# The squared activations of two MLPs turned by VectorE in 32x32 blocks instead of by TensorE

## The chip, the cores and the metric

One Trainium2 chip, one core. The metric is the device time of one execution in microseconds; of several runs the median is taken.

## The reference, cut to what matters

The program computes three transformer layers on 256 tokens of width 2048 in float32. The change lies in the MLPs of the first two layers, which have this form:

```python
def sq_relu_mlp(h, w1, w2):          # h: 256 x 2048, w1: 2048 x 8192, w2: 8192 x 2048
    a = jax.nn.relu(jnp.einsum("btd,df->btf", h, w1))
    return jnp.einsum("btf,fd->btd", a * a, w2)

# for each of two layers
x = x + rms_norm(m, mix_post_g[layer])        # m: output of the layer's mixer
h = rms_norm(x, ffn_pre_g[layer])
x = x + rms_norm(sq_relu_mlp(h, ffn_w1[layer], ffn_w2[layer]), ffn_post_g[layer])
```

Around them stand a pooling and convolution mixer (before the first MLP), a short convolution (between them), and a third layer with attention and gating (behind the second).

## The kernel before

All large products go the same way. The activations are the stationary operand, 128x128, with the features on the partitions; the weights are the moving operand, 128 rows x 512 columns; a product of 256 tokens x 512 columns is a *chunk* and fills two PSUM banks, one for each tile of 128 tokens. Both operands are kept as a sum of two fp32r parts, hi and lo, and each product is three matmuls: hi by lo, lo by hi and hi by hi (lines 687 to 689, `step_matmuls`). A chunk is worked in *steps* of two feature tiles, 12 matmuls each. There are 960 steps in one list, `SEQ`; `POS` gives a step's place in it and `S_END` the place behind a chunk's last step.

SyncE loads weights two steps at a time into three slots of w_raw. For each step ScalarE rounds the raw weights to w_hi (`split_hi`, line 666) and VectorE subtracts it from the raw ones into w_lo (`split_lo`, line 673). There are six slots for the split weights. Each engine has its own program, in which the steps of `SEQ` follow each other in a loop (`split_steps`); at step s ScalarE and VectorE first split the weights of step s+3, and then do what else belongs to step s. TensorE's loop (`matmul_steps`) waits for the split weights and for the stationary operand, issues the 12 matmuls, and then does what else belongs to the step.

An MLP goes in 8 blocks of 1024 hidden features. A block has two *up* chunks of 8 steps (j = 0, 1, with w1, stationary operand A) and four *down* chunks of 4 steps (with w2, stationary operand B). They are ordered so that the up chunks of block b+1 come ahead of the down chunks of block b: up 0, up 1, down 0, up 2, down 1, and so on, up 7, down 6, down 7. In block 0 the two up chunks are interleaved. For an up chunk

- ScalarE takes the banks at the chunk's last step, with the ReLU and the tokens' scale, into one of three slots of z (`to_z`, line 958): 128 tokens on the partitions, 512 features, for each of the two token tiles;
- GpSimd squares them in place (`pool_mlp`, line 1870);
- at the second step behind the chunk TensorE waits for the squares (`squared`) and turns them: eight transpositions of 128x128 by an identity (`turn_z` and `turn`, line 732), four into each of two of the four small PSUM banks, 4 to 7 (`aux_bank`); these are used in turn by every such piece of work of the program, in the order that `aux_order` lists, and TensorE waits for a bank to be free (`aux_free`);
- at the same step of their own programs ScalarE casts the two banks into B_hi (`hi_plain`, line 993), and VectorE, behind it, subtracts B_hi from the banks into B_lo (`lo_plain`, line 1353). A later `wait_step` of TensorE waits for `lo_cast`.

B has room for 16 feature tiles, so two blocks. Down chunks are added into `acc`: those of block 0 are copied by ScalarE (`copy_acc`), those of blocks 1 to 6 are added by VectorE at the chunk's last step (line 1633). The buffer `conv_out` is used by the mixers and by the attention, and by nothing in the MLPs.

Of the kernel before, what the change touches and what calls it, by code (L numbers as in the profile page):

```python
# [13 lines left out]
TOK = 256  # L14
# [25 lines left out]
Z_SLOTS = 3  # L40
TAP_SLOTS = 2
STEP_K = 2
AHEAD = 3
# [29 lines left out]
def up_chunk(layer, b, j):  # L73
    return (C_M0, C_M1)[layer] + (j if b == 0 else 2 + 6 * (b - 1) + j)
# [106 lines left out]

def aux_order():
    two = range(2)
    yield from [("first",)]
    yield from [("pre", 0, g, h) for g in range(NG) for h in two]
    yield from [("rows",)]
    yield from [("vg", q) for q in range(4)]
    for j in two:
        yield from [("win", j, h) for h in two] + [("mix", j, h) for h in two]
    yield from [("ln", tt, h) for tt in two for h in two]  # L190
    yield from [("silu", j, h) for j in two for h in two]
    for layer in two:
        yield from pre_fills(1 + 2 * layer)
        yield from [("h", layer, b, j, h) for b in range(NB) for j in two for h in two]
        if layer == 0:
            yield from pre_fills(2)
            for j in range(NG):
                yield from [("cu", j, h) for h in two] + [("bg", j, h) for h in two]
    yield from pre_fills(4)
    yield from [("qk", r, h) for r in range(4) for h in two]  # L200
    yield from [("ws", h) for h in two]
    for r in range(8, 14):
        for i in range(8):
            if (r, i) in ((11, 1), (13, 1)):
                yield from [("sgu", (r - 11) // 2, tt) for tt in two]
            if (r, i) == (12, 3):
# [29 lines left out]
def build(nc, t):  # L236
    ctx = ExitStack()
    with ctx:
# [6 lines left out]
        def signal(name, keys):  # L245
            return Signal(semaphore(name), list(keys))
# [23 lines left out]
        S0 = [POS[c, 0] for c in range(N_CHUNKS)] + [STEPS]  # L270
        S_END = [POS[c, n_steps[c] - 1] + 1 for c in range(N_CHUNKS)]
        STEPS_PER_LOAD = GK // STEP_K
        LOADS = STEPS // STEPS_PER_LOAD

# [43 lines left out]
        att = conv_out_flat[:, 0:NT * W_ATT].rearrange("p (t c) -> p t c", t=NT)  # L318
        vg = conv_in_flat[:, 0:NT * W_ATT].rearrange("p (t c) -> p t c", t=NT)
        ws_T = ws_flat.rearrange("p (g c) -> p g c", g=HEADS)  # L320
        scores = scores_flat.rearrange("p (s c) -> p s c", s=2)
# [49 lines left out]

        aux = list(aux_order())
        AUX_N = {k: n for n, k in enumerate(aux)}
        CAST = [k for k in aux if k[0] in ("pre", "mix", "silu", "h", "bg", "ao", "zb", "merged")]

# [27 lines left out]
        for p in range(4):  # L403
# [6 lines left out]
                                   ([(g, tt) for tt in tiles for g in gs] if 0 in gs else [(g, tt) for g in gs for tt in tiles])])  # L410
        tap_done = signal("tap_done", DVE_TAPS)
        ln_bias = signal("ln_bias", [(tt,) for tt in tiles])
        ln_stats = signal("ln_stats", [(tt, h) for tt in tiles for h in two])
# [36 lines left out]
        def aux_done(key):  # L450
# [3 lines left out]
            if kind == "rows":  # L454
                return par_made.sem, par_made.of("rows", 3)
            if kind in ("pre", "mix", "h", "ao", "zb", "merged"):
                return lo_cast.sem, lo_cast.of(*key)
# [21 lines left out]
        def z_done(key):  # L479
# [3 lines left out]
            if kind == "v":  # L483
                return aux_filled.sem, aux_filled.of("vg", *rest)
            by_pe = {"u": "win", "p": "mix", "c": "cu", "b": "bg", "qk": "qk", "ub": "zb", "h": "h", "ws": "ws"}
            if kind in by_pe:
# [145 lines left out]
        def since(c, i, before):  # L632

            return POS[c, i] - S_END[before]

# [81 lines left out]
        def pe_program(e):  # L717
# [102 lines left out]

            boundary(1)
            pe_mlp(e, turn_x, turn_z, 0)
            boundary(2)

# [12 lines left out]
            boundary(3)  # L837
            pe_mlp(e, turn_x, turn_z, 1)
            boundary(4)
# [68 lines left out]

        def pe_mlp(e, turn_x, turn_z, layer):
# [37 lines left out]
        def act_program(e):  # L947
# [150 lines left out]
            boundary(1)  # L1098
            act_mlp(e, at, to_z, hi_plain, copy_acc, squares, early, 0)
            boundary(2)  # L1100
# [31 lines left out]
            boundary(3)  # L1132
            act_mlp(e, at, to_z, hi_plain, copy_acc, squares, early, 1)
            boundary(4)


            for c, i in split_steps(e, 4, split_hi, at):
                r = c - C_L2
                if i == n_steps[c] - 1:
# [7 lines left out]
                    elif r < 8:  # L1147
                        j = r - 6
                        act_sigmoids(e, r, lambda tt: att[:, tt, j * CH:(j + 1) * CH],
                                     (lo_cast.sem, lo_cast.of("bg", NG - 1, 1)))  # L1150
                    elif r < 10:
# [116 lines left out]

        def act_mlp(e, at, to_z, hi_plain, copy_acc, squares, early, layer):
            p = 1 + 2 * layer  # L1270
            for c, i in split_steps(e, p, split_hi, at):
# [45 lines left out]
        def dve_program(e):  # L1317
# [132 lines left out]
            boundary(1)  # L1450
            dve_mlp(e, at, lo_plain, finish_last, early, 0)
            boundary(2)
# [29 lines left out]
            boundary(3, True)  # L1482
            dve_mlp(e, at, lo_plain, finish_last, early, 1)
            boundary(4)
# [135 lines left out]

        def dve_mlp(e, at, lo_plain, finish_last, early, layer):
            p = 1 + 2 * layer
            for c, i in split_steps(e, p, split_lo, at):
# [13 lines left out]
                for b in range(NB):  # L1637
                    for j in two:
                        if since(c, i, up_chunk(layer, b, j)) == 1:
                            lo_plain("B", (2 * b + j) % NG, "h", layer, b, j)  # L1640

        def short_conv(e, j):
            if j > 0:
                e.wait_ge(lo_cast.sem, lo_cast.of("bg", j - 1, 1))
            e.wait_ge(conv_fed.sem, conv_fed.of("cu", j, 1))
# [268 lines left out]
```

## Time and profile before

| | |
|---|---|
| median of 3 runs | 2739.95 us (2738.39 to 2740.3) |
| the profiled execution, its own time | 2737.03 us |
| its span | 2735.3 us |
| TensorE (PE) busy | 2720.4 us, 99% |
| VectorE (DVE) busy | 1535.3 us, 56% |
| ScalarE (ACT) busy | 1294.2 us, 47% |
| GpSimd (POOL) busy | 278.3 us, 10% |
| DMA, mean over the span | 188 GB/s |

All rows come from one profiled execution. PE is TensorE's matmul side and PEld its loading of the stationary operand, which lies beside it. In a group of instructions, "x960" is their number, then come their busy time in us and the mean of one in ns, and behind the bar the idle time of the engine just ahead of them and what ended it. In a timeline a line gives start, time and instruction; "x4" merges four neighbours, and the bracket is the idle time ahead of them. Neighbouring instructions of an engine overlap a little, and matmuls by much, so that a distance between starts says more of a cost than a duration. A transposition by TensorE appears as a MATMUL with `ident`. The row of a block's busy times gives, behind the stretch and its length, the busy us (and the instructions) of PE, PEld, DVE, ACT and POOL, then TensorE's granted clock, the mean busy share of the DMA engines, and GB/s.

### The profile page before, as it was taken

The page shows a single profiled execution, that of the slowest core. Times are in us where ns is not written, and L with a number is a line of the kernel's source. Part 1 is how long each engine was busy: PE and PEld are TensorE (multiplying, and loading weights), DVE is VectorE, ACT ScalarE, POOL GpSimd, SP SyncE. Part 2 cuts the span into 40 slices and gives each one's busy share as a digit, 9 for nine tenths or more (in the row PEclk, how much of TensorE's full clock was granted, in tenths as well). Part 3 has the DMA queues.
Part 4 walks back from the last instruction along what each step waited for, and adds up shares of the span by engine and source line. Part 5 has one row for each costly group of instructions (what it writes and reads, how often), then busy time and mean ns, then how long its engine had stood idle before and what let it go on. Part 6 is the DMA issues. An engine that isn't in the chain of part 4 may idle for free.

```text
span 2735.3 us, 31039 instructions
## 1 busy us (share of the span) xinstructions
PE 2720.4 (99%) x12357; PEld 2257.1 (83%) x12357; DVE 1535.3 (56%) x1727; ACT 1294.2 (47%) x1639; POOL 278.3 (10%) x263
## 2 busy tenths in 40 slices
PE   8999999999999999999999999999999999999999
PEld 7888888888888888888888888888888888888887
DVE  6887545445554565555654554455565557644454
ACT  6765544434444454444544444344445446543442
POOL 4751000000000010000110000000011001100000
PEclk9999999999999999999999999999999999999999
DMA  7545655555555555555555555555555555455554
GB/s 245 188 160 192 206 197 177 193 185 185 187 190 189 190 182 200 185 185 206 194 180 198 199 177 193 193 185 185 186 184 185 193 185 182 160 204 193 185 185 154
DMA packets 267632, 515.57 MB, mean 188 GB/s; under 512 B 8370, under 2 KB 27364, under 8 KB 266980
## 3 DMA queue, kind: packets, MB, share of 16 engines
q1 hardware_dynamic: 267492, 513.60, 54.6%
q8 instruction: 101, 1.65, 0.2%
q14 instruction: 39, 0.32, 0.0%
HBM read 511.47 MB, written 2.10 MB: 188 GB/s over the span
## 4 chain that ended last, share of the span: by engine, by line
PE 95%; issue 2%; DVE 1%; ACT 1%; DMA 1%; POOL 1%; SPq 0%; POOLq 0%; DVEq 0%; ACTq 0%
PE bank L687 30%; PE bank L689 30%; PE bank L688 30%; PE bank L732 2%; DVE w_lo L673 1%; POOL acc L1751 0%; ACT w_hi L666 0%; ACT bank L1009 0%; PE bank L905 0%; DMA w_raw<-in_sc_w_in 0%; DMA w_raw<-in_ffn_w 0%; DMA w_raw<-in_w_in 0%; DVE acc L1370 0%; POOL small L1745 0%; DMA tap_product<-in_mix_pre_g 0%
## 5 line engine op out<-in xcount | busy, mean ns | idle before, releaser
L673 DVE TENSOR_TENSOR w_lo<-w_raw,w_hi 128x1024 fp32r<-128x1024 f32 x960 | 1175.8, 1267 | 702.5 <-ACT w_hi L666 696.4
L666 ACT ACTIVATE w_hi<-w_raw 128x1024 fp32r<-128x1024 f32 x960 | 978.4, 1058 | 617.2 <-PE bank L689 506.8
L687 PE MATMUL bank<-w_hi,A_lo 128*128 128x512 f32 x2432 | 955.5, 393 | 3.5 <-DVE w_lo L673 3.2
L689 PE MATMUL bank<-w_hi,A_hi 128*128 128x512 f32 x2432 | 948.1, 390 | 0.0
L688 PE MATMUL bank<-w_lo,A_hi 128*128 128x512 f32 x2432 | 947.7, 390 | 0.0
L687 PE MATMUL bank<-w_hi,B_lo 128*128 128x512 f32 x1408 | 550.2, 391 | 0.0
L689 PE MATMUL bank<-w_hi,B_hi 128*128 128x512 f32 x1408 | 548.0, 389 | 0.0
L688 PE MATMUL bank<-w_lo,B_hi 128*128 128x512 f32 x1408 | 547.9, 389 | 0.0
L687 PEld LDWEIGHTS bank<-w_hi,A_lo 128*128 128x128 f32 x2432 | 457.3, 188 | 97.5 <-DVE w_lo L673 5.2
L689 PEld LDWEIGHTS bank<-w_hi,A_hi 128*128 128x128 f32 x2432 | 457.1, 188 | 95.8
L688 PEld LDWEIGHTS bank<-w_lo,A_hi 128*128 128x128 f32 x2432 | 457.5, 188 | 92.5
L689 PEld LDWEIGHTS bank<-w_hi,B_hi 128*128 128x128 f32 x1408 | 264.3, 188 | 54.8
L687 PEld LDWEIGHTS bank<-w_hi,B_lo 128*128 128x128 f32 x1408 | 264.4, 188 | 54.2
L688 PEld LDWEIGHTS bank<-w_lo,B_hi 128*128 128x128 f32 x1408 | 264.4, 188 | 54.0
L958 ACT ACTIVATE z<-bank,small 128x512 f32<-128x512 f32 x108 | 68.4, 686 | 327.8 <-PE bank L689 327.7
L1870 POOL TENSOR_TENSOR z<-z 128x512 f32<-128x512 f32 x64 | 65.2, 1040 | 1132.3 <-ACT z L958 1132.3
L1633 DVE TENSOR_TENSOR acc<-bank,acc 128x512 f32<-128x512 f32 x96 | 61.9, 686 | 199.5 <-PE bank L689 199.5
L1751 POOL TENSOR_TENSOR acc<-acc,gain_row 128x512 f32<-128x512 f32 x32 | 41.0, 1297 | 512.9 <-ACT bank L1009 491.6
L993 ACT ACTIVATE B_hi<-bank 128x512 fp32r<-128x512 f32 x72 | 39.2, 596 | 97.7 <-PE bank L732 97.7
L1353 DVE TENSOR_TENSOR B_lo<-bank,B_hi 128x512 fp32r<-128x512 f32 x72 | 46.4, 686 | 48.9 <-ACT B_hi L993 48.9
L1745 POOL TENSOR_TENSOR small<-small,neg_half 128x1 f32<-128x1 f32 (+2 forms) x21 | 23.3, 1110 | 330.3 <-DVE small L1321 330.3
L1009 ACT ACTIVATE bank<-acc 128x512 f32<-128x512 f32 x32 | 19.0, 595 | 77.5 <-DVE acc L1370 51.3
(155 smaller groups left out, 893.3 us busy)
## 6 DMA issues: line engine op xcount, KB each, us to landing
w_raw<-in_ffn_w SPq DMA_DIRECT2D x256, 1024.0 KB, 5.4
w_raw<-in_w_in SPq DMA_DIRECT2D x88, 1024.0 KB, 5.1
w_raw<-in_sc_w_in SPq DMA_DIRECT2D x48, 1024.0 KB, 5.2
w_raw<-in_ab_w_in SPq DMA_DIRECT2D x32, 512.0 KB, 5.2
w_raw<-in_ab_w_out SPq DMA_DIRECT2D x16, 1024.0 KB, 5.0
w_raw<-in_sc_w_out SPq DMA_DIRECT2D x16, 1024.0 KB, 5.3
w_raw<-in_w_out SPq DMA_DIRECT2D x16, 1024.0 KB, 5.3
w_raw<-in_ab_w_in SPq DMA_DIRECT2D x8, 1024.0 KB, 5.1
```

What stands on the lines that cost most here:

```text
L666: e.activation(w_hi[:, s % SPLIT_SLOTS, :], raw, ACT.Copy).then_inc(hi_made, 1)
L673: e.tensor_tensor(w_lo[:, slot, :], raw, w_hi[:, slot, :].bitcast(F32), ALU.subtract).then_inc(lo_made, 1)
L687: e.matmul(ps, lo[:, kt, tok], wh, start=first, stop=False)
L688: e.matmul(ps, hi[:, kt, tok], wl, start=False, stop=False)
L689: ins = e.matmul(ps, hi[:, kt, tok], wh, start=False, stop=last)
L732: ins = e.transpose(view[:, k, tt * P:(tt + 1) * P], src(tt, slice(f, f + P)), ident)
L958: e.activation(out(tt), main_bank(c, tt), func, scale=rs(layer_of(c))[:, tt:tt + 1]).then_inc(act_took(c, tt), 1)
L993: e.activation(halves[buf][0][:, kt:kt + 2, :], view, ACT.Copy).then_inc(hi_cast(*key, h), 1)
L1353: e.tensor_tensor(lo[:, kt:kt + 2, :], aux_bank(*key, h).rearrange("p (k t) -> p k t", k=2), hi[:, kt:kt + 2, :].bitcast(F32), ALU.subtrac ...
L1633: e.tensor_tensor(out, main_bank(c, tt), out, ALU.add).then_inc(dve_took(c, tt), 1)
L1751: e.tensor_tensor(out, out, gain_row[:, c], ALU.mult).then_inc(gained(p, n, tt), 1)
L1870: e.tensor_tensor(z[:, s, tt, :], z[:, s, tt, :], z[:, s, tt, :], ALU.mult).then_inc(squared(layer, b, j, tt), 1)
```

## The change

TensorE no longer turns the squares of the MLPs, and their 64 fillings of the small banks are gone from the order of these banks. VectorE turns them with its own transposition, which turns 32x32 blocks, from z to a view `h_T` of `conv_out` (features on the partitions, 4 tiles x 256 tokens). A transposition takes one group of 32 token partitions and one group of 32 features of each feature tile, for both token tiles and all four feature tiles, 32 partitions x 256 elements, and writes it to the 32 partitions of these features. 16 of them make a chunk's turn. They are spread over eight steps of VectorE's program, two in each (`turn_hidden`), from a step on that `TURN_AT` gives: the second step behind the up chunk (its place in the list is `S_END` + 1, as before), or later if the turn before isn't over. The first of them waits for the squares, and for the remainders of the turn before (which read `h_T`). In the step behind the eighth, ScalarE casts `h_T` to B_hi and VectorE subtracts into B_lo, now both from SBUF. `z`'s slots come free, and the first uses of `conv_out` behind each MLP begin, by the new signals.

```diff
+TURN_STEPS = 8
...
+        TURN_AT = {}
+        for layer in range(2):
+            free = 0
+            for b in range(NB):
+                for j in range(2):
+                    TURN_AT[layer, b, j] = max(free, S_END[up_chunk(layer, b, j)] + 1)
+                    free = TURN_AT[layer, b, j] + TURN_STEPS + 1
...
+        h_T = conv_out_flat[:, 0:GK * TOK].rearrange("p (k t) -> p k t", k=GK)
...
-        aux = list(aux_order())
+        aux = [key for key in turn_order() if key[0] != "h"]
...
+            if kind == "h":
+                return turned.sem, turned.of(*rest)
...
         def pe_mlp(e, turn_x, layer):
...
-                for b in range(NB):
-                    for j in two:
-                        if since(c, i, up_chunk(layer, b, j)) == 1:
-                            e.wait_ge(squared.sem, squared.of(layer, b, j, 1))
-                            turn_z(z_slot("h", layer, b, j), "h", layer, b, j)
...
         def act_mlp(e, at, to_z, copy_acc, squares, early, layer):
...
-                        if since(c, i, up_chunk(layer, b, j)) == 1:
-                            hi_plain("B", (2 * b + j) % NG, "h", layer, b, j)
+                        if POS[c, i] == TURN_AT[layer, b, j] + TURN_STEPS:
+                            e.wait_ge(turned.sem, turned.of(layer, b, j))
+                            for h in two:
+                                kt = GK * ((2 * b + j) % NG) + 2 * h
+                                e.activation(halves["B"][0][:, kt:kt + 2, :], h_T[:, 2 * h:2 * h + 2, :],
+                                             ACT.Copy).then_inc(hi_cast("h", layer, b, j, h), 1)
...
+        def turn_hidden(e, layer, b, j, n):
+            s = z_slot("h", layer, b, j)
+            quarters = [divmod(m, 4) for m in range(16 * n // TURN_STEPS, 16 * (n + 1) // TURN_STEPS)]
+            if n == 0:
+                e.wait_ge(squared.sem, squared.of(layer, b, j, 1))
+                if (b, j) != (0, 0):
+                    before = (b, j - 1) if j > 0 else (b - 1, 1)
+                    e.wait_ge(lo_cast.sem, lo_cast.of("h", layer, *before, 1))
+            for q, r in quarters:
+                tok, feat = slice(32 * q, 32 * q + 32), slice(32 * r, 32 * r + 32)
+                src = z[tok, s, :, :].rearrange("p t (k c) -> p t k c", k=GK)[:, :, :, feat]
+                dst = h_T[feat, :, :].rearrange("p k (t c) -> p t k c", t=NT)[:, :, :, tok]
+                ins = e.transpose(dst, src)
+            if n == TURN_STEPS - 1:
+                ins.then_inc(turned(layer, b, j), 1)
...
         def dve_mlp(e, at, finish_last, early, layer):
...
-                        if since(c, i, up_chunk(layer, b, j)) == 1:
-                            lo_plain("B", (2 * b + j) % NG, "h", layer, b, j)
+                        n = POS[c, i] - TURN_AT[layer, b, j]
+                        if 0 <= n < TURN_STEPS:
+                            turn_hidden(e, layer, b, j, n)
+                        if n == TURN_STEPS:
+                            for h in two:
+                                kt = GK * ((2 * b + j) % NG) + 2 * h
+                                e.wait_ge(hi_cast.sem, hi_cast.of("h", layer, b, j, h))
+                                e.tensor_tensor(halves["B"][1][:, kt:kt + 2, :], h_T[:, 2 * h:2 * h + 2, :],
+                                                halves["B"][0][:, kt:kt + 2, :].bitcast(F32),
+                                                ALU.subtract).then_inc(lo_cast("h", layer, b, j, h), 1)
```

## Rows read from the trace of the kernel before

**Rows 1.** The page: busy time by engine, granted TensorE clock, and the chain of waits.
```profile
PE 2720.4 (99%) x12357; PEld 2257.1 (83%) x12357; DVE 1535.3 (56%) x1727; ACT 1294.2 (47%) x1639; POOL 278.3 (10%) x263
...
PEclk9999999999999999999999999999999999999999
...
PE 95%; issue 2%; DVE 1%; ACT 1%; DMA 1%; POOL 1%; SPq 0%; POOLq 0%; DVEq 0%; ACTq 0%
```

**Rows 2.** TensorE's waits for others, whole kernel: total us, times, longest.
```profile
PE bank L687 <- DVE w_lo L673: 3.2, 1, 3.2
```

**Rows 3.** The same in 270:970 (first MLP), then in 1345:2050 (second).
```profile
PE bank L749 <- DVE x_res L1384: 0.7, 1, 0.7
...
PE bank L749 <- DVE x_res L1384: 0.5, 1, 0.5
```

**Rows 4.** Groups of instructions by line and shape, whole kernel.
```profile
L673 DVE TENSOR_TENSOR w_lo<-w_raw,w_hi 128x1024 fp32r<-128x1024 f32 x960 | 1175.8, 1267 | 702.5 <-ACT w_hi L666 696.4
L666 ACT ACTIVATE w_hi<-w_raw 128x1024 fp32r<-128x1024 f32 x960 | 978.4, 1058 | 617.2 <-PE bank L689 506.8 <-DMA w_raw<-in_sc_w_in 35.4 <-DMA w_raw<-in_ffn_w 27.1
...
L732 PE MATMUL bank<-ident,z 128*128 128x128 f32 x384 | 49.7, 272 | 0.0
...
L1353 DVE TENSOR_TENSOR B_lo<-bank,B_hi 128x512 fp32r<-128x512 f32 x72 | 46.4, 686 | 48.9 <-ACT B_hi L993 48.9
...
L993 ACT ACTIVATE B_hi<-bank 128x512 fp32r<-128x512 f32 x72 | 39.2, 596 | 97.7 <-PE bank L732 97.7
```

**Rows 5.** Timeline of TensorE around one turn: start us, duration us, instruction.
```profile
508.18 0.39 PE L689 MATMUL bank<-w_hi,A_hi 128*128 128x512 f32 x1
508.41 1.03 PE L732 MATMUL bank<-ident,z 128*128 128x128 f32 x8
509.20 0.48 PE L687 MATMUL bank<-w_hi,A_lo 128*128 128x512 f32 x1
509.51 0.40 PE L688 MATMUL bank<-w_lo,A_hi 128*128 128x512 f32 x1
```

**Rows 6.** Timeline of VectorE in the same block.
```profile
505.49 2.78 DVE L673 TENSOR_TENSOR w_lo<-w_raw,w_hi 128x1024 fp32r<-128x1024 f32 x2 [8.11 <-ACT w_hi L666]
...
548.47 1.29 DVE L1633 TENSOR_TENSOR acc<-bank,acc 128x512 f32<-128x512 f32 x2 [5.05 <-PE bank L689]
549.67 4.62 DVE L673 TENSOR_TENSOR w_lo<-w_raw,w_hi 128x1024 fp32r<-128x1024 f32 x4
559.35 1.29 DVE L1633 TENSOR_TENSOR acc<-bank,acc 128x512 f32<-128x512 f32 x2 [5.05 <-PE bank L689]
```

**Rows 7.** Timeline of GpSimd in the same block and the next.
```profile
504.01 2.04 POOL L1870 TENSOR_TENSOR z<-z 128x512 f32<-128x512 f32 x2 [64.13 <-ACT z L958]
526.66 2.04 POOL L1870 TENSOR_TENSOR z<-z 128x512 f32<-128x512 f32 x2 [20.61 <-ACT z L958]
592.84 2.04 POOL L1870 TENSOR_TENSOR z<-z 128x512 f32<-128x512 f32 x2 [64.13 <-ACT z L958]
```

**Rows 8.** Groups by line and shape: other float32 work of VectorE on SBUF.
```profile
L1654 DVE SCALAR_TENSOR_TENSOR conv_out<-conv_in,par,conv_out 128x256 f32<-128x256 f32 x32 | 13.0, 487 | 0.0
...
L1479 DVE TENSOR_TENSOR B_lo<-conv_out,B_hi 128x512 fp32r<-128x512 f32 x8 | 5.5, 692 | 5.6 <-ACT B_hi L1129 5.6
...
L1651 DVE TENSOR_SCALAR conv_out<-conv_in,par 128x256 f32<-128x256 f32 x16 | 4.7, 353 | 13.5 <-ACT conv_in L1122 13.5
...
L1506 DVE TENSOR_TENSOR z<-z,conv_in 128x1024 f32<-128x1024 f32 x2 | 2.5, 1226 | 0.1
...
L1724 DVE TENSOR_REDUCE small<-scores 128x1 f32<-128x128 f32 x8 | 2.3, 286 | 0.3
```

**Rows 9.** Busy time by engine in one block (columns as told above).
```profile
504.01:592.84 88.83, 88.83 (x402) 73.75 (x401) 45.79 (x44) 37.44 (x41) 4.08 (x5) 1.00 0.55 190
```

**Rows 10.** Timeline of ScalarE at the end of the same up chunk.
```profile
503.24 1.27 ACT L958 ACTIVATE z<-bank,small 128x512 f32<-128x512 f32 x2 [7.12 <-PE bank L689]
```

**Rows 11.** Groups by line and shape: ScalarE's cast into B_hi from SBUF.
```profile
L1129 ACT ACTIVATE B_hi<-conv_out 128x512 fp32r<-128x512 f32 x8 | 5.1, 633 | 18.9 <-DVE conv_out L1475 18.9
```

More of the change, by code:

```diff
@@ L178, in pre_fills, with turn_order @@
            [("pre", p, g, h) for g in range(2, NG) for h in range(2)]
-def aux_order():
+def turn_order():
     two = range(2)
@@ L370, in evicted_by @@
             return "ACT" if r < 30 and (r - 14) % 4 < 2 else "DVE"
-        aux = list(aux_order())
+        aux = [key for key in turn_order() if key[0] != "h"]
         AUX_N = {k: n for n, k in enumerate(aux)}
-        CAST = [k for k in aux if k[0] in ("pre", "mix", "silu", "h", "bg", "ao", "zb", "merged")]
+        CAST = [k for k in turn_order() if k[0] in ("pre", "mix", "silu", "h", "bg", "ao", "zb", "merged")]
         tile0_done = signal("tile0_done", [(c,) for c in by_token])
@@ L411, in build @@
         tap_done = signal("tap_done", DVE_TAPS)
+        turned = signal("turned", [(l, b, j) for l in two for b in range(NB) for j in two])
         ln_bias = signal("ln_bias", [(tt,) for tt in tiles])
@@ L455, in aux_done @@
                 return par_made.sem, par_made.of("rows", 3)
-            if kind in ("pre", "mix", "h", "ao", "zb", "merged"):
+            if kind in ("pre", "mix", "ao", "zb", "merged"):
                 return lo_cast.sem, lo_cast.of(*key)
@@ L484, in z_done @@
                 return aux_filled.sem, aux_filled.of("vg", *rest)
-            by_pe = {"u": "win", "p": "mix", "c": "cu", "b": "bg", "qk": "qk", "ub": "zb", "h": "h", "ws": "ws"}
+            by_pe = {"u": "win", "p": "mix", "c": "cu", "b": "bg", "qk": "qk", "ub": "zb", "ws": "ws"}
+            if kind == "h":
+                return turned.sem, turned.of(*rest)
             if kind in by_pe:
@@ L821, in pe_program @@
             boundary(1)
-            pe_mlp(e, turn_x, turn_z, 0)
+            pe_mlp(e, turn_x, 0)
             boundary(2)
@@ L837, in pe_program @@
             boundary(3)
-            pe_mlp(e, turn_x, turn_z, 1)
+            pe_mlp(e, turn_x, 1)
             boundary(4)
@@ L907, in mix_pooled, with pe_mlp @@
                 ins.then_inc(aux_filled("mix", j, h), 1)
-        def pe_mlp(e, turn_x, turn_z, layer):
+        def pe_mlp(e, turn_x, layer):
             p = 1 + 2 * layer
@@ L1098, in act_program @@
             boundary(1)
-            act_mlp(e, at, to_z, hi_plain, copy_acc, squares, early, 0)
+            act_mlp(e, at, to_z, copy_acc, squares, early, 0)
             boundary(2)
@@ L1132, in act_program @@
             boundary(3)
-            act_mlp(e, at, to_z, hi_plain, copy_acc, squares, early, 1)
+            act_mlp(e, at, to_z, copy_acc, squares, early, 1)
             boundary(4)
@@ L1149, in act_program @@
                         act_sigmoids(e, r, lambda tt: att[:, tt, j * CH:(j + 1) * CH],
-                                     (lo_cast.sem, lo_cast.of("bg", NG - 1, 1)))
+                                     (lo_cast.sem, lo_cast.of("h", 1, NB - 1, 1, 1)))
                     elif r < 10:
@@ L1267, in act_silu, with act_mlp @@
                 e.activation(halves["B"][0][:, kt:kt + 2, :], silu_parts(h)[0], ACT.Copy).then_inc(hi_cast("silu", j, h), 1)
-        def act_mlp(e, at, to_z, hi_plain, copy_acc, squares, early, layer):
+        def act_mlp(e, at, to_z, copy_acc, squares, early, layer):
             p = 1 + 2 * layer
@@ L1450, in dve_program @@
             boundary(1)
-            dve_mlp(e, at, lo_plain, finish_last, early, 0)
+            dve_mlp(e, at, finish_last, early, 0)
             boundary(2)
@@ L1482, in dve_program @@
             boundary(3, True)
-            dve_mlp(e, at, lo_plain, finish_last, early, 1)
+            dve_mlp(e, at, finish_last, early, 1)
             boundary(4)
@@ L1619, in dve_silu, with dve_mlp @@
                                 ALU.subtract).then_inc(lo_cast("silu", j, h), 1)
-        def dve_mlp(e, at, lo_plain, finish_last, early, layer):
+        def turn_hidden(e, layer, b, j, n):
[13 more added lines that the diff above has]
+                ins.then_inc(turned(layer, b, j), 1)
+        def dve_mlp(e, at, finish_last, early, layer):
             p = 1 + 2 * layer
@@ L1638, in dve_mlp @@
                     for j in two:
-                        if since(c, i, up_chunk(layer, b, j)) == 1:
-                            lo_plain("B", (2 * b + j) % NG, "h", layer, b, j)
+                        n = POS[c, i] - TURN_AT[layer, b, j]
[8 more added lines that the diff above has]
+                                                ALU.subtract).then_inc(lo_cast("h", layer, b, j, h), 1)
         def short_conv(e, j):
-            if j > 0:
-                e.wait_ge(lo_cast.sem, lo_cast.of("bg", j - 1, 1))
+            e.wait_ge(lo_cast.sem, lo_cast.of("bg", j - 1, 1) if j > 0 else lo_cast.of("h", 0, NB - 1, 1, 1))
             e.wait_ge(conv_fed.sem, conv_fed.of("cu", j, 1))
```

## The prediction, made before the change was run

> **What bounds the kernel now.** I read the page first. TensorE is busy for 99% of the span and carries 95% of the chain of waits; its granted clock is 1.0 in all forty slices, the 2.4 GHz level [rows 1]. Over the whole kernel TensorE waited longest for another engine in one wait of 3.2 us for a w_lo [rows 2]; in the stretches of the two MLPs its list of waits has a single entry each, 0.7 and 0.5 us, for the x that a stage boundary turns [rows 3]. So in the two MLP stages every microsecond of TensorE work is a microsecond of the kernel, and nothing else is. The list of groups then gives the work beside it: the splits of the weights on ScalarE (L666) and VectorE (L673), and what is to be changed, the turns (L732 reading z), the casts into B_hi (L993) and the remainders into B_lo (L1353) [rows 4].
>
> **What the change removes on TensorE.** There are 2 layers x 8 blocks x 2 chunks = 32 turns of a squared chunk, each of 8 transpositions: 256 of the 384 instructions of the z row of L732 [rows 4]. (The other 128 belong to the mixers and the attention and stay.) The mean of 272 ns is a pipelined duration, so the price must be read as a delay. In the timeline the last weight matmul starts at 508.18, the eight transpositions at 508.41, the next L687 at 509.20 and the L688 behind it at 509.51 [rows 5]. From 508.41 to 509.51 is 1.10 us, of which one L687 needs about 0.23 us (508.18 to 508.41) anyway: 0.87 us a turn. A second reading goes by distances. Between two evictions of down chunks, at 548.47 and 559.35, lie 4 steps without a turn: 10.88 us, 2.72 us a step [rows 6]. GpSimd squares a chunk at 504.01, the next at 526.66 and the same chunk of the next block at 592.84 [rows 7]. The first distance, 22.65 us, is 8 steps (21.76) and one turn: 0.89 us. The second, 88.83 us, is 32 steps (87.04) and two turns: 1.79 us, 0.895 us each. I take 0.895 us, since it holds every after-effect on the matmuls behind the turn. 32 x 0.895 = 28.6 us. The bounds are 0.79 us (508.41 to 509.20) and 1.03 us (the busy time of the eight), so 25.3 to 33.0 us. TensorE also loses a wait for the squares and one for a free small bank, which cost nothing now [rows 3].
>
> The Trainium skill speaks here ("VectorE: DVE Perf Modes", section "The three transpose paths"): it puts a TensorE transposition of 128x128 at 390 ns, and its table of rules says to use TensorE for it if PSUM may take the result. By its figure the 256 would be an estimated 100 us; the trace shows 0.895 us for eight, 0.11 us each, so the measured distance decides. Its advice against VectorE is right on engine time, as the next part finds, but engine time of VectorE isn't what the span is made of.
>
> **What it adds on VectorE.** For each turn 16 transpositions of 32 partitions x 256 elements, two in each of eight steps: 512 in all. The trace has no transposition on VectorE. The nearest rows are f32 operations from SBUF to SBUF: 692 ns for 512 elements a partition and 1226 ns for 1024, so 1.04 ns an element and 158 ns fixed, which gives 425 ns for 256; a three-operand one with 256 elements takes 487 ns and a one-input one 353 ns [rows 8]. I take T = 0.43 us, by the element count, and keep as ends 0.29 us (a 128x128 reduction) and 1.23 us (the 1024-element row: what it costs if a transposition takes four times as long an element) [rows 8]. 512 x 0.43 = 220 us of VectorE, 13.8 us a block of 88.83 us. A block has 45.79 us of VectorE work in it now [rows 9], so it would go to 59.6 us of 87.0: it fits.
>
> The mean isn't enough, since the transpositions come in a burst ahead of the splits that TensorE needs soon. I count steps from E, the first after the first up chunk of a block. The turns fill steps E+1 to E+8 and E+10 to E+17, with the remainders at E+9 and E+18. At the start of the burst the trace shows ScalarE's two evictions at 503.24, as TensorE ends the chunk [rows 10], and two w_lo of VectorE from 505.49, done at 508.27 [rows 6]. TensorE wants the second of these after four more steps, at 503.2 + 10.9 = 514.1: a lead of 5.8 us. From E+1 to E+17 TensorE takes 17 x 2.72 = 46.2 us. VectorE has in that time 17 splits at 1.16 us (four in a row take 4.62 [rows 6]), two pairs of evictions of 1.2 (548.47 to 549.67), one pair of remainders of about the same, and 32 T: 23.3 + 32 T. It keeps up as long as 23.3 + 32 T < 46.2 + 5.8, that is up to T = 0.90 us, twice what I take. Within a single step the load is 1.16 + 0.86 = 2.02 us against 2.72, so the lead grows rather than shrinks; in a down chunk that VectorE evicts it is 4 x 2.02 + 1.2 = 9.3 us against 10.88. The cost on the path is 0.
>
> **What moves.** The casts of ScalarE go from the step behind the chunk to 8 steps later and read SBUF: 633 ns rather than 596 [rows 4, 11], 64 x 0.04 = 2.4 us more on an engine that idles 617 us ahead of its splits alone [rows 4]; 0 on the path. ScalarE now waits there for VectorE's last transposition, and the w_hi of four steps on is queued behind it. That takes about 4.4 us from the chunk's end to the last transposition (evictions 1.3, a w_hi 1.06, a w_lo 1.16, two transpositions 0.86), then 1.3 of casts, 1.06 of w_hi and 1.16 of w_lo: 7.9 us, for a w_lo that is wanted 13.6 us after that end. VectorE's new wait for the squares is met: they are done at 504.01 + 2.04 = 506.05 and VectorE comes there at 508.27 [rows 6, 7]. B is wanted later than it is filled: from block 1 on the last cast is at E+18 and the down chunk begins at E+24. Block 0 is tightest: its second remainder stands at step 30 and is read at step 34, of which VectorE's place in the order gives away nothing, since it splits three steps ahead: some 8 us of cover. The slots of z are held 8 steps longer, and each is written again over 20 steps later. DMA issues, GpSimd and the order of the splits don't change. The transfers only have to come 1% faster in the MLPs, at a DMA share of 0.55 there [rows 9].
>
> **The sum.** The profiled execution took 2737.03 us with a span of 2735.3, and is 2.9 us below the median of the runs. By its own time 2737.0 - 28.6 = 2708.4; by the median 2739.95 - 28.6 = 2711.3 us, which I forecast.
>
> **Rivals.**
> A. VectorE becomes the bound in the burst. Place: the splits that the down chunks after the second up chunk wait for. From T = 0.90 us it costs 32 x (T - 0.90) us a block, and from T = 0.96 more than the 1.79 us a block that it saves. At the upper end of 1.23 it is 10.6 us a block, 16 x 10.6 = 170 us: 2711 + 170 = 2881 us. For it: no row shows the operation. Against: the f32 rows of 256 elements take 353 and 487 ns, and this would need twice the longer one [rows 8]. Chance 0.07.
> B. Part of the gain is given back: T just at 0.93, or the first block of each layer or a stage boundary makes TensorE wait for a w_lo as it did once for 3.2 us. At T = 0.93 it is 32 x 0.03 = 1.0 us a block, 16 us in all: about 2727 us. Chance 0.05, a fifth of it within the bound of no change.
> C. The turns were cover for something that is late next, a weight transfer or a w_hi, so that TensorE waits as long as it turned before: 2740 us. For it: ScalarE waits 27 us for transfers of the MLP weights [rows 4]. Against: these waits are hidden behind leads of several steps, and no weight matmul of the MLPs waits for anything [rows 3]. Chance 0.03.
> D. Each transposition is worth its full 272 ns: 256 x 0.272 = 70 us, 2670 us. For it: the rows' duration [rows 4]. Against: the distances from block to block [rows 7]. Chance 0.01. The skill's 390 ns, named above, would be this rival at an estimated 2640 us.
>
> **How the numbers follow.** My forecast has 0.84. Its own range is 2711 with the bounds of the turn's price, 2707 to 2715, and a microsecond or two of scatter between medians. Below 2705 only D lies. For the range I go to 2720, into B; 0.13 or so is left out. A measurement of this kernel can tell about 0.2%, 5.5 us, from no change. Faster: 0.84 + 0.04 (B) + 0.01 (D) = 0.89. Same: 0.01 (B) + 0.03 (C) = 0.04. Slower: 0.07 (A).
>
> **What would show it.** In the profile of the changed kernel: the row of TensorE's transpositions of z has 128 instructions rather than 384, and there are 512 transpositions of 32x256 on VectorE with a mean near 430 ns; the mean itself decides A. The distance between squares of one chunk in two blocks falls from 88.83 to 87.0 us. TensorE's waits have no new entry in the MLPs. VectorE's busy time goes from 1535 to about 1755 us, and the wait of its w_lo for w_hi shrinks by about the same. I am wrong if the distance stays above 88, if TensorE waits for w_lo, or if the distance falls and the time doesn't.

## The result, and the profile after

The changed kernel takes 2710.66 us (median of 4 runs, 2709.59 to 2712.24), the kernel before 2739.74 us beside it: 29.1 us less, ratio 0.9895 with a 95% interval of 0.9878 to 0.9912, which is 24 to 33 us. Forecast were 2711.3 us and 28.6 us less.

The page of the changed kernel, its parts that answer to [rows 1]:

```profile
PE 2692.3 (99%) x12101; PEld 2231.2 (82%) x12101; DVE 1768.7 (65%) x2239; ACT 1296.7 (48%) x1639; POOL 278.2 (10%) x263
...
PEclk9999999999999999999999999999999999999999
...
PE 94%; issue 2%; DVE 1%; DMA 1%; ACT 1%; POOL 1%; SPq 0%; POOLq 0%; DVEq 0%
```

TensorE has 256 instructions fewer and 28.1 us less to do, and the span is 26.4 us shorter. VectorE has 233 us more to do, and the chain that ends last hardly passes over it.

The clock is the upper level, 2.4 GHz, in all but 3 to 4 us of the span. A 9 in the row of the clock stands for 0.9 or more in a slice of 68 us, so a short fall doesn't show there. In this execution TensorE waited 2.91 us for x_res ahead of the first MLP, and its granted clock was 0.60 from 253 to 254 us, 0.50, the 1.2 GHz level, from 254 to 256, and 0.69 in the microsecond after that. In the profiled execution of the kernel before the same wait was 1.41 us, and in that of a second run of the changed kernel 1.67 us; in both the clock stayed at 1.00. That is why the two spans differ by 26.4 us and not by 28.6: GpSimd's first square of the first MLP stands at 294.13 us, 2.2 us later than before (291.90), ahead of every turn. From there to the last square of the second MLP are 1637.44 us, and were 1665.21: 27.77 us less for the 31 turns between them, 0.896 each.

The groups that answer to [rows 4]. Line numbers have moved: L687 is the w_lo, L680 the w_hi, L1648 the new transposition, L1677 and L1299 the remainder and the cast, and L746 TensorE's transpositions of z:

```profile
L687 DVE TENSOR_TENSOR w_lo<-w_raw,w_hi 128x1024 fp32r<-128x1024 f32 x960 | 1191.6, 1268 | 587.7 <-ACT w_hi L680 582.4
L680 ACT ACTIVATE w_hi<-w_raw 128x1024 fp32r<-128x1024 f32 x960 | 977.6, 1056 | 574.7 <-PE bank L703 399.9 <-DMA w_raw<-in_ffn_w 82.4 <-DMA w_raw<-in_sc_w_in 35.3
...
L1648 DVE STREAM_TRANSPOSE conv_out<-z 32x256 f32<-32x256 f32 x512 | 223.1, 436 | 10.5
...
L1677 DVE TENSOR_TENSOR B_lo<-conv_out,B_hi 128x512 fp32r<-128x512 f32 x64 | 41.2, 686 | 5.5 <-ACT B_hi L1299 5.5
...
L1299 ACT ACTIVATE B_hi<-conv_out 128x512 fp32r<-128x512 f32 x64 | 37.1, 628 | 100.7 <-DVE conv_out L1648 100.7
...
L746 PE MATMUL bank<-ident,z 128*128 128x128 f32 x128 | 16.6, 273 | 0.0
```

The new operation takes 436 ns, 512 times. The remainders cost what they cost before, 686 ns, from SBUF instead of PSUM; ScalarE's casts take 628 ns in place of 596 (633 was forecast). TensorE's waits, over the whole kernel and in the two MLPs, beside [rows 2, 3]:

```profile
PE bank L763 <- DVE x_res L1397: 4.1, 3, 2.9
PE bank L701 <- DVE w_lo L687: 3.3, 1, 3.3
...
PE bank L763 <- DVE x_res L1397: 0.7, 1, 0.7
...
PE bank L763 <- DVE x_res L1397: 0.6, 1, 0.6
```

There is no new entry. The waits for x_res at the stage boundaries, of which the 2.91 us above is the longest, were shorter in the profile before:

```profile
PE bank L749 <- DVE x_res L1384: 2.6, 3, 1.4
```

GpSimd's squares, as in [rows 7], give the length of a block:

```profile
500.85 2.04 POOL L1908 TENSOR_TENSOR z<-z 128x512 f32<-128x512 f32 x2 [63.24 <-ACT z L967]
522.61 2.04 POOL L1908 TENSOR_TENSOR z<-z 128x512 f32<-128x512 f32 x2 [19.72 <-ACT z L967]
587.89 2.04 POOL L1908 TENSOR_TENSOR z<-z 128x512 f32<-128x512 f32 x2 [63.24 <-ACT z L967]
```

From 500.85 to 587.89 are 87.04 us, which is 32 steps of 2.72 and nothing else; it was 88.83. From 500.85 to 522.61 are 21.76 us, eight steps without a turn; it was 22.65. In that block VectorE is busy for 60.40 us, where [rows 9] had 45.79:

```profile
500.85:587.89 87.04, 87.04 (x386) 72.07 (x385) 60.40 (x76) 37.47 (x41) 4.08 (x4) 1.00 0.57 194
```

And this is how the burst runs on VectorE, from the split behind the first up chunk on:

```profile
502.33 2.77 DVE L687 TENSOR_TENSOR w_lo<-w_raw,w_hi 128x1024 fp32r<-128x1024 f32 x2 [8.11 <-ACT w_hi L680]
505.03 0.87 DVE L1648 STREAM_TRANSPOSE conv_out<-z 32x256 f32<-32x256 f32 x2
505.92 1.23 DVE L687 TENSOR_TENSOR w_lo<-w_raw,w_hi 128x1024 fp32r<-128x1024 f32 x1
507.18 0.89 DVE L1648 STREAM_TRANSPOSE conv_out<-z 32x256 f32<-32x256 f32 x2
508.08 1.23 DVE L687 TENSOR_TENSOR w_lo<-w_raw,w_hi 128x1024 fp32r<-128x1024 f32 x1
...
526.68 1.23 DVE L687 TENSOR_TENSOR w_lo<-w_raw,w_hi 128x1024 fp32r<-128x1024 f32 x1
527.83 1.29 DVE L1677 TENSOR_TENSOR B_lo<-conv_out,B_hi 128x512 fp32r<-128x512 f32 x2
...
532.64 1.29 DVE L1664 TENSOR_TENSOR acc<-bank,acc 128x512 f32<-128x512 f32 x2 [0.36 <-PE bank L703]
```

Two transpositions stand between two w_lo, and a step takes 508.08 - 505.92 = 2.16 us of VectorE against 2.72 of TensorE: VectorE gains on TensorE in the burst. At 527.83 are the remainders of the first turn, right behind a split, without a wait for ScalarE's casts; at 532.64 VectorE waits for TensorE to end a down chunk.

### The profile page after: what moved, and what is told of

Its sections match the earlier page's. It is cut to its first block, busy times and chain, and to the rows that moved or that the text cites. A ratio compares the mean times of both kernels' runs of the same rounds, so it can differ in the third digit from the quotient of the medians.

```text
span 2708.9 us, 31038 instructions
## 1 busy us (share of the span) xinstructions
PE 2692.3 (99%) x12101; PEld 2231.2 (82%) x12101; DVE 1768.7 (65%) x2239; ACT 1296.7 (48%) x1639; POOL 278.2 (10%) x263
## 4 chain that ended last, share of the span: by engine, by line
PE 94%; issue 2%; DVE 1%; DMA 1%; ACT 1%; POOL 1%; SPq 0%; POOLq 0%; DVEq 0%
PE bank L701 31%; PE bank L703 31%; PE bank L702 31%; PE bank L746 1%; DVE w_lo L687 1%; POOL acc L1789 0%; ACT w_hi L680 0%; ACT bank L1018 0%; PE bank L919 0%; DMA w_raw<-in_ffn_w 0%; DMA w_raw<-in_ab_w_in 0%; DMA w_raw<-in_sc_w_in 0%; DMA w_raw<-in_w_in 0%; DVE acc L1383 0%; POOL small L1783 0%
## 5 line engine op out<-in xcount | busy, mean ns | idle before, releaser
L687 DVE TENSOR_TENSOR w_lo<-w_raw,w_hi 128x1024 fp32r<-128x1024 f32 x960 | 1191.6, 1268 | 587.7 <-ACT w_hi L680 582.4
L680 ACT ACTIVATE w_hi<-w_raw 128x1024 fp32r<-128x1024 f32 x960 | 977.6, 1056 | 574.7 <-PE bank L703 399.9
L1648 DVE STREAM_TRANSPOSE conv_out<-z 32x256 f32<-32x256 f32 x512 | 223.1, 436 | 10.5
L1664 DVE TENSOR_TENSOR acc<-bank,acc 128x512 f32<-128x512 f32 x96 | 61.9, 686 | 85.7 <-PE bank L703 85.7
L1299 ACT ACTIVATE B_hi<-conv_out 128x512 fp32r<-128x512 f32 x64 | 37.1, 628 | 100.7 <-DVE conv_out L1648 100.7
```

What stands on the lines that cost most here:

```text
L680: e.activation(w_hi[:, s % SPLIT_SLOTS, :], raw, ACT.Copy).then_inc(hi_made, 1)
L687: e.tensor_tensor(w_lo[:, slot, :], raw, w_hi[:, slot, :].bitcast(F32), ALU.subtract).then_inc(lo_made, 1)
L1299: e.activation(halves["B"][0][:, kt:kt + 2, :], h_T[:, 2 * h:2 * h + 2, :], ACT.Copy).then_inc(hi_cast("h", layer, b, j, h), 1)
L1648: ins = e.transpose(dst, src)
L1664: e.tensor_tensor(out, main_bank(c, tt), out, ALU.add).then_inc(dve_took(c, tt), 1)
```

## The experiments

Theory 1 is that of the prediction: the gain is TensorE's time for the turns, whole, and VectorE's transpositions are free as long as its lead over TensorE covers their burst. Each run stands beside runs of the kernel before on the same chip (2738.4 to 2739.5 us); a second run of the changed kernel gave 2709.79 us (ratio 0.9892, 0.9877 to 0.9907).

**TensorE's turns put back beside VectorE's.**

```diff
-        aux = [key for key in turn_order() if key[0] != "h"]
+        aux = list(turn_order())
...
         def pe_mlp(e, turn_x, turn_z, layer):
...
+                        if since(c, i, up_chunk(layer, b, j)) == 1:
+                            e.wait_ge(squared.sem, squared.of(layer, b, j, 1))
+                            turn_z(z_slot("h", layer, b, j), "h", layer, b, j)
```

> The changed kernel with TensorE's 32 turns put back at their old place (eight transpositions each, after the wait for the squares, into the small banks in the old order), while VectorE's turns stay and are the ones that are read; nothing reads what TensorE turns. Theory 1 (the gain is TensorE's time for the turns and nothing else): 32 x 0.895 = 28.6 us come back, 2739 us, level with the kernel before. Theory 2 (part of the gain came from what hung on the turns: casts out of PSUM, waits for small banks): it stays below the kernel before by that part, 2715 to 2733 us. Theory 3 (VectorE's transpositions cost time of their own that the gain outweighed): it comes out above the kernel before, over 2745 us.

It took 2740.22 us, ratio 0.9999 to the kernel before (0.9990 to 1.0008). GpSimd's squares show the old length of a block:

```profile
505.50 2.04 POOL L1915 TENSOR_TENSOR z<-z 128x512 f32<-128x512 f32 x2 [64.13 <-ACT z L974]
528.16 2.04 POOL L1915 TENSOR_TENSOR z<-z 128x512 f32<-128x512 f32 x2 [20.61 <-ACT z L974]
594.33 2.04 POOL L1915 TENSOR_TENSOR z<-z 128x512 f32<-128x512 f32 x2 [64.13 <-ACT z L974]
```

594.33 - 505.50 = 88.83 us, to the hundredth what it was, with VectorE's 512 transpositions still there:

```profile
L1655 DVE STREAM_TRANSPOSE conv_out<-z 32x256 f32<-32x256 f32 x512 | 223.1, 436 | 10.5
```

So the whole gain is TensorE's time for the turns, and neither the casts out of PSUM nor the casts' and remainders' hold on the small banks had a share in it: in this kernel both read what VectorE turned, and a small bank is free as soon as TensorE has filled it. Theories 2 and 3 fall.

**No turn at all.**

```diff
-            for q, r in quarters:
+            for q, r in (quarters[-1:] if n == TURN_STEPS - 1 else []):
```

> The changed kernel without the turns on VectorE: of the 16 transpositions of a chunk only the last is left, so that h_T is mostly not filled and the products of the MLPs are not the reference's; the casts, remainders and waits stay. Theory 1 (VectorE's 220 us lie wholly beside TensorE): same time as the changed kernel, 2710.7 us within 2 us, with VectorE's busy time down by about 209 us. Theory 3 (they cost something): faster by what they cost, under 2706 us.

It took 2710.39 us (ratio 0.9893, 0.9877 to 0.9908), the changed kernel's time, with 221 us less of VectorE work; 480 transpositions of 436 ns would be 209, and the splits account for the rest (L687 went from 1191.6 to 1178.3 us):

```profile
PE 2693.4 (99%) x12101; PEld 2231.9 (82%) x12101; DVE 1547.3 (57%) x1759; ACT 1297.7 (48%) x1639; POOL 278.2 (10%) x263
...
L1648 DVE STREAM_TRANSPOSE conv_out<-z 32x256 f32<-32x256 f32 x32 | 14.1, 441 | 1.0
```

VectorE's turns cost the kernel no time that these runs can tell.

**Twice, two and a half times and three times the transpositions.** These look for the point from which rival A decides.

```diff
             for q, r in quarters:
...
+                spare = (conv_out_flat[:, GK * TOK:2 * GK * TOK], conv_in_flat[:, 8 * (TOK + CONV_K - 1) - GK * TOK:])
+                for extra in spare[:1]:            # [:1 + r % 2] for two and a half, [:2] for three
+                    e.transpose(extra..., src)
                 ins = e.transpose(dst, src)
```

> The changed kernel with each transposition of the turns issued a second time, into memory that nothing reads: T is 0.87 us where 0.43 was. Theory 1 (in a burst VectorE keeps up until 23.3 + 32 T reaches 52.0 us, T = 0.90): just no loss, 2711 us, at most 2716, while VectorE gets some 223 us more of work. Rival (the bound is the sum in a single step, 1.16 + 2 T < 2.72, T = 0.78, with no lead that carries over): 32 x 0.09 x 16 = 46 us more, about 2757 us.

> The changed kernel with each transposition issued three times, two of them into memory that nothing reads: T is 1.31 us. Theory 1: 32 x (1.31 - 0.90) = 13.1 us a block, 16 blocks, 210 us: about 2921 us, with TensorE waiting for w_lo inside each block. Rival (no lead that carries over, break-even at 0.78): 32 x 0.53 x 16 = 271 us, about 2982 us. If VectorE were bound only by its mean load over a block (45.8 + 32 T against 87 us, T = 1.29), it would be 2720 us at most.

Twice as many took 2709.13 us (ratio 0.9888, 0.9875 to 0.9902): no loss, as theory 1 has it. Three times took 2844.95 us (ratio 1.0384, 1.0370 to 1.0398): the loss is there, and TensorE waits for w_lo,

```profile
PE bank L701 <- DVE w_lo L687: 90.1, 141, 3.1
```

but it is 135 us where 210 were forecast. The list of waits holds only a part of it: in the block below TensorE is idle for 5.7 us, and its busy time is 89.72 us in place of 87.04, 2.7 more, at a granted clock of 1.00.

```profile
527.37:622.75 95.38, 89.72 (x386) 71.38 (x385) 80.75 (x140) 36.64 (x41) 4.08 (x5) 1.00 0.53 177
```

Part of VectorE's timeline in that kernel shows why the loss is smaller than forecast:

```profile
535.00 0.43 DVE L1650 STREAM_TRANSPOSE conv_out<-z 32x256 f32<-32x256 f32 x1
535.36 0.39 DVE L1650 STREAM_TRANSPOSE conv_in<-z 32x256 f32<-32x256 f32 x1
535.69 0.39 DVE L1652 STREAM_TRANSPOSE conv_out<-z 32x256 f32<-32x256 f32 x1
536.10 0.44 DVE L1650 STREAM_TRANSPOSE conv_out<-z 32x256 f32<-32x256 f32 x1
...
537.20 1.23 DVE L687 TENSOR_TENSOR w_lo<-w_raw,w_hi 128x1024 fp32r<-128x1024 f32 x1
538.46 0.43 DVE L1650 STREAM_TRANSPOSE conv_out<-z 32x256 f32<-32x256 f32 x1
...
540.66 1.23 DVE L687 TENSOR_TENSOR w_lo<-w_raw,w_hi 128x1024 fp32r<-128x1024 f32 x1
```

Six transpositions and a split go from 537.20 to 540.66, 3.46 us; by their durations they would be 6 x 0.41 + 1.23 = 3.7, and I had put 6 x 0.436 + 1.16. The starts of transpositions lie 0.33 to 0.41 us apart, since one that reads the same source as the one ahead begins before that has ended; and a split ahead of a transposition takes 1.26 us, not the 1.16 of a row of splits. The sum of the prediction, with distances in place of durations: 17 x 1.26 + 3.6 + 16 x 2.20 = 60.2 us of VectorE in the burst, against 52.0, so 8.2 us a block. From block to block of that kernel lie

```profile
527.37 2.04 POOL L1912 TENSOR_TENSOR z<-z 128x512 f32<-128x512 f32 x2 [71.57 <-ACT z L967]
...
622.75 2.04 POOL L1912 TENSOR_TENSOR z<-z 128x512 f32<-128x512 f32 x2 [71.58 <-ACT z L967]
```

95.38 us, 8.34 more than 87.04. With this corrected sum the run between the two was forecast before it was made:

> The changed kernel with two and a half times the transpositions (each twice, every second one three times, the added ones into memory that nothing reads). The run with three times showed 0.365 us from start to start and 1.26 us for a split ahead of a transposition; by these distances the burst takes 17 x 1.26 + 3.6 + 16 x 5 x 0.37 = 54.6 us against 46.2 + 5.8 = 52.0. Theory 1 with these distances: 2.6 us a block, 42 us in all, 2752 us. With the durations in their place, as in the prediction (T = 1.09): 23.3 + 34.9 = 58.2, 6.2 us a block, 2810 us. Rival (there is no lead that carries over, a step of 1.26 + 1.85 = 3.11 us against 2.72): 16 x 16 x 0.39 = 100 us, 2810 us as well; it is told apart by the run with twice as many, where it wants no loss only below 1.46 us a step.

It took 2762.81 us (ratio 1.0086, 1.0069 to 1.0103), 11 us more than the 2752 expected; the form with durations wanted 2810. Its block, and that of the kernel with twice as many:

```profile
509.69 2.04 POOL L1912 TENSOR_TENSOR z<-z 128x512 f32<-128x512 f32 x2 [65.31 <-ACT z L967]
...
599.85 2.04 POOL L1912 TENSOR_TENSOR z<-z 128x512 f32<-128x512 f32 x2 [65.32 <-ACT z L967]
```

```profile
498.65 2.04 POOL L1912 TENSOR_TENSOR z<-z 128x512 f32<-128x512 f32 x2 [63.24 <-ACT z L967]
...
585.69 2.04 POOL L1912 TENSOR_TENSOR z<-z 128x512 f32<-128x512 f32 x2 [63.24 <-ACT z L967]
```

90.16 us is 3.12 more than 87.04, where 2.6 was forecast (its step is 3.13 us, not 3.11, which gives 2.9); 87.04 is no loss. The four kernels stand together:

| transpositions | VectorE's step in the burst | VectorE's burst, worked out | loss a block, worked out | measured |
|---|---|---|---|---|
| once | 2.16 | 39 | none | none |
| twice | 2.81 | 50 | none | none |
| 2.5 times | 3.13 | 54.9 | 2.9 | 3.12 |
| three times | 3.46 | 60.2 | 8.2 | 8.34 |

In this table the row of three times is no test, since its distances come from that run; the test is the row of 2.5. Both losses are 0.1 to 0.2 us a block above the sum. The kernel with one burst, below, shows where a part of it can lie: there the step that wants the split is due at 520.52, which is 5 steps less 0.3 us behind the start of ScalarE's eviction at 507.20, so the lead of 5.8 us that the sum takes from that start is 5.5. With it the sum gives 3.2 and 8.5 us.

The rival without a lead that carries over wants (2.81 - 2.72) x 16 = 1.4 us a block at twice as many, 23 us in all, and falls: the block didn't grow at all. The one by the mean load alone wants next to nothing at three times, and falls as well.

**The whole turn in one step, and in two.**

```diff
-TURN_STEPS = 8
+TURN_STEPS = 1                                   # 2 in the second kernel
```

> The changed kernel with all 16 transpositions of a turn in one step of VectorE's program (TURN_STEPS = 1) in place of eight, so about 7.1 us in which no weight is split. Theory 1 (what counts is whether VectorE's lead covers the burst): the w_lo behind the burst is done 5.1 + 7.1 + 1.2 = 13.4 us after the up chunk's end and wanted after 13.6: just no loss, 2711 us. Rival (the spreading over eight steps is what makes it free): each burst makes TensorE wait 1 us or more, 32 us in all, 2743 us or more.

It took 2728.59 us (ratio 0.9959, 0.9945 to 0.9974): 18.8 us more than the changed kernel beside it (2709.79 us), neither what I nor what the rival expected. The burst itself is as worked out:

```profile
509.44 2.77 DVE L687 TENSOR_TENSOR w_lo<-w_raw,w_hi 128x1024 fp32r<-128x1024 f32 x2 [8.11 <-ACT w_hi L680]
512.14 7.17 DVE L1648 STREAM_TRANSPOSE conv_out<-z 32x256 f32<-32x256 f32 x16
519.34 1.23 DVE L687 TENSOR_TENSOR w_lo<-w_raw,w_hi 128x1024 fp32r<-128x1024 f32 x1
```

The split behind it ends at 520.57, 13.4 us after the chunk's end (ScalarE's eviction starts at 507.20), and was to be in time by 0.2 us. It is late by a little: TensorE's last matmul ahead of it starts at 520.29, and the next at 520.62, where 520.52 was its turn. Blocks take 87.54 us, 0.5 more, 8 us in all. What I had not worked out is the first block of each layer, whose two up chunks end 4 steps apart and not 8. VectorE comes to the second burst without a lead, and TensorE waits 3.5 us in each layer:

```profile
PE bank L701 <- DVE w_lo L687: 3.5, 1, 3.5
```

Together that is what the squares show: from the first of the first MLP to the last of the second are 1652.59 us, and 1637.72 in the second run of the changed kernel, 14.9 us more. Another 3.0 us lie ahead of the first MLP and have nothing to do with the turns (first square at 296.24 against 293.25): TensorE waited 2.8 us for x_res there, and its granted clock from 250 to 260 us was 0.84 (0.83 in the profile after above, 1.00 in that of the second run). That is one execution; the others have no profile. Two bursts were then tried:

> The changed kernel with eight transpositions in each of two steps (TURN_STEPS = 2). The run with one burst lost 0.26 us a turn and 3.5 us more in the first block of each layer, whose two up chunks end only 4 steps apart. Theory 1 (a burst costs only what it overruns VectorE's lead by): 3.6 us a burst; the w_lo behind the first is done 5.1 + 3.6 + 1.2 = 9.9 us after the up chunk's end and wanted after 13.6, the one behind the second 14.7 and wanted after 16.3: no loss, 2710 us. Rival (any burst of more than a step's free 1.5 us costs): 2720 us or more.

They took 2711.64 us (ratio 0.9901, 0.9885 to 0.9918): 1 to 2 us above the changed kernel, with two short waits of TensorE for a w_lo, 0.8 us each, in the first block of each layer. Four times as many transpositions in a step as in the changed kernel are nearly free.

**What a transposition is paid by.**

```diff
-            for q, r in quarters:
-                tok, feat = slice(32 * q, 32 * q + 32), slice(32 * r, 32 * r + 32)
-                src = z[tok, s, :, :]...[:, :, :, feat]
-                dst = h_T[feat, :, :]...
+            for q, r in [(m, m) for m in range(4 * n // TURN_STEPS, 4 * (n + 1) // TURN_STEPS)]:
+                src = z[:, s, :, :]...[:, :, :, feat]
+                dst = h_T...
```

> The changed kernel with four transpositions of all 128 partitions x 256 elements for each turn, one in every second step, in place of 16 of 32 partitions: each turns the same 32x32 blocks of its own 32 partitions, so that blocks stay in their group of partitions and the products of the MLPs are not the reference's. It asks what a transposition is paid by. If by elements a partition (as the other operations of VectorE): 0.436 us each, 56 us of VectorE in all, and the same time, 2710 us. If the four groups of 32 partitions are paid one by one: 1.3 to 1.7 us each. The kernel's time tells nothing here; the mean of the row does.

This ran once (2712.31 us), and only the row matters:

```profile
L1648 DVE STREAM_TRANSPOSE conv_out<-z 128x256 f32<-128x256 f32 x128 | 55.5, 434 | 0.0
```

434 ns for 128 partitions, as for 32: the price doesn't grow with the partitions. That it goes by the elements a partition is what the forecast of 0.43 us assumed; no run has another number of elements than 256. The row agrees with the Trainium skill ("Vector Engine (DVE) Microarchitecture Reference", section 3.8, the reshape front-end), which puts a 32x32 array in front of each 32-channel bank of VectorE, four in all.

**The mixer's turns moved as well.** If TensorE's time is all that counts, its other turns should be worth as much each. Eight of them stand in the short convolution's stage.

```diff
-        aux = [key for key in turn_order() if key[0] != "h"]
+        aux = [key for key in turn_order() if key[0] not in ("h", "cu", "bg")]
...
-                    turn_z(z_slot("c", j), "cu", j)
...
-                    turn_z(z_slot("b", j - 1), "bg", j - 1)
...
+                    if i < 4:
+                        ins = turn_blocks(e, z_slot("c", j), short_in[:, :, SPAD:], range(4 * i, 4 * i + 4))
...
+                    per = 8 if j == NG else 2
...
+                    if per * i < 16:
+                        ins = turn_blocks(e, z_slot("b", j - 1), bg_T, range(per * i, per * i + per))
```

> The changed kernel with the eight turns of the short convolution's stage also moved from TensorE to VectorE (four of c times u, straight into the convolution's input, four transpositions a step; four of b, beside the convolution's output, two a step, and eight a step for the last, which is wanted at once). Theory 1 (a turn of TensorE is worth 0.9 us wherever TensorE is never idle, and VectorE's are free while its lead lasts): 8 x 0.895 = 7.2 us less, 2703.5 us, ratio to the changed kernel 0.9974. Rival (the last turn, which stands right ahead of its use, makes TensorE wait, and the bursts of four a step beside the convolution's 4.4 us use up the lead): at most 3 us less, or more time than the changed kernel, with waits of TensorE for w_lo or B_lo in this stage.

It took 2702.76 us (ratio to the kernel before 0.9867, 0.9852 to 0.9882), and the changed kernel beside it 2709.79: 7.0 us less, with 7.2 forecast. It beats both kernels. The four times of each kernel don't overlap (2702.07 to 2703.45 us, and 2708.47 to 2710.28). The added rows, and TensorE's only wait for a w_lo in the whole kernel, which was there before:

```profile
L1652 DVE STREAM_TRANSPOSE conv_out<-z 32x256 f32<-32x256 f32 x64 | 27.9, 436 | 1.2
...
L1652 DVE STREAM_TRANSPOSE conv_in<-z 32x256 f32<-32x256 f32 x64 | 27.9, 436 | 1.0
```

```profile
PE bank L710 <- DVE w_lo L696: 3.3, 1, 3.3
```

Bursts of four and even eight in a step fit, where the end of a chunk gives VectorE its lead and nothing else is in the way.

## Why the prediction was right

**The term on the path** was read twice from distances, 0.87 and 0.895 us a turn. A block is now 1.79 us shorter, 0.895 a turn; times 32 it is 28.6, and with TensorE's turns put back the time is the old one. The medians came within 0.6 us of the forecast, closer than an interval of 24 to 33 us can tell; the distances are what bears the term out. The 272 ns of a transposition's row would have given 70 us (rival D). The 390 ns that the Trainium skill has for it ("VectorE: DVE Perf Modes", section "The three transpose paths"; its figure is for bf16, and these are float32) would have given an estimated 100 us; no run here shows such a price, with 0.11 us each in a row of eight.

**VectorE's transposition** had no row. T was worked out as 0.43 us and is 0.436. VectorE's work in a block was forecast as 59.6 us and is 60.40. That it came so near is in part luck: the trace before had only other operations to read T from, and left it 0.29 to 1.23 us.

**Its cover** was forecast as sufficient up to T = 0.90 us. This number was mis-sized, in a way that didn't matter here: it mixed a duration (T) with a distance taken where no transposition follows (1.16 for a split). By distances alone the limit is (52.0 - 17 x 1.26 - 3.6) / 32 = 0.84 us, and the changed kernel is at 0.45. Rival A, as a mechanism, is real: it is what the runs with more transpositions show, and its price past the limit is 32 us a block for each us of T, as written. With three times the transpositions it was 135 us and not the 210 expected. Rival B's place in the first block of a layer is real too, but only for a turn in one burst.

**What moves.** The casts, B's filling and z's slots gave nothing away: no wait of TensorE is new [rows 3]. One sign was read off by half: I had expected the idle time of w_lo ahead of w_hi to shrink by VectorE's added 220 us. It shrank by 115 (702.5 to 587.7 us), and the other half came out of VectorE's waits for TensorE at the down chunks, 199.5 us before and 85.7 after. The remainders' waits for casts went from 48.9 to 5.5 us. Rival C had in its favour that ScalarE waits for weight transfers. These waits did grow, from 27 to 82 us, and to 193 us with twice the transpositions:

```profile
L680 ACT ACTIVATE w_hi<-w_raw 128x1024 fp32r<-128x1024 f32 x960 | 971.2, 1055 | 523.4 <-PE bank L703 240.4 <-DMA w_raw<-in_ffn_w 193.3 <-DMA w_raw<-in_sc_w_in 35.5
```

A slot of w_raw is free when VectorE has split it, so the later VectorE is, the later the load starts. At twice the transpositions this is still hidden behind six slots of split weights.

## What to carry to other kernels

Where one engine is busy for 99% of the span and hardly waits, price what is taken off it by the distance between repeated events with and without it, not by an instruction's duration: 0.895 us for eight transpositions of 272 ns each. The work may cost the other engine eight times as much (16 x 0.44 us here) and still be free, but it has to be spread so that the engine's lead at each place covers it: add up that engine's distances over the burst, against the bound engine's time plus the lead at its start, and look at the places where two bursts come close. Then look for the same work elsewhere: eight more turns gave another 7 us.

## What the runs showed of the hardware

- VectorE's transposition of 32x32 blocks in float32 takes 436 ns for 256 elements a partition, with 32 partitions (into any other 32) or with 128 (434 ns). Behind another one that reads the same source it takes 394 ns and starts 0.33 to 0.37 us later; the next one, with a new source, starts 0.41 us later. Where every one has a source of its own, the starts lie 0.45 us apart (7.2 us for 16).
- A split of 128x1024 takes 1.26 us from start to start ahead of a transposition, and 1.16 in a row of splits.
- GpSimd's squares and VectorE's splits hold each other up, and the transpositions don't take part in that. Two squares take 2.04 us in the changed kernel, as before, and the split that starts while they run takes 1.64 us in place of 1.23 (at 524.09 us in the profile after). With two and a half times the transpositions a split starts at 531.41 us, just ahead of the squares at 531.45, and the two squares take 3.08 us. With three times as many, only transpositions start from 548.83 us until a split at 551.04, and the two squares at 549.13 take 2.04 us.
- TensorE's granted clock fell to 0.50 for 2 us in one profiled execution of the changed kernel, behind a wait of 2.91 us; behind waits of 1.41 and 1.67 us at the same place it stayed at 1.00.
